# Moving the transfers that prepare the paired weights, and building the input sums in another place and on another engine

## The reference, cut to what matters

```python
def conv_ffn(x, prev, w_gate, w_up, w_dw, w_down):
    g = x @ w_gate
    g_ext = jnp.concatenate([prev.astype(g.dtype), g], axis=1)
    g_c = depthwise_causal_conv(g_ext, w_dw)
    y = (jax.nn.gelu(g_c, approximate=True) * (x @ w_up)) @ w_down
    return y, g_ext[:, -(FFN_CONV_WIDTH - 1):]
...
    f, st_f = conv_ffn(rms_norm(h, p['norm_ffn_pre'][layer]), ffn_prev[layer], ...)
    h = h + rms_norm(f, p['norm_ffn_post'][layer])
```

## Time and profile before

| | |
|---|---|
| median of 3 runs | 3144.06 us (3136.15 to 3147.18) |
| the profiled execution | 3141.24 us, span of the trace 3139.5 us |
| PE busy | 3004.6 us, 96% of the span |
| DVE, ACT, POOL busy | 1922.6, 1431.9, 518.0 us |
| granted PE clock, mean | 0.98 |
| transfers | 739.67 MB, mean 236 GB/s |
| queue of SP (q1), of POOL (q0) | 589.87 MB, 145.60 MB |

### The profile page before, as it was taken

The page is one execution under the profiler, slowest core; times in us unless marked ns, Lnnn a source line. Parts: engine busy times, 40 slices in busy tenths (PEclk is TensorE's granted clock), DMA queues, the critical chain, the costliest instruction groups (busy, mean ns, idle before and its releaser), DMA issues.

```text
span 3139.5 us, 62628 instructions
## 1 busy us (share of the span) xinstructions
PE 3004.6 (96%) x24274; PEld 2598.1 (83%) x24274; DVE 1922.6 (61%) x2846; ACT 1431.9 (46%) x2709; POOL 518.0 (16%) x738
## 2 busy tenths in 40 slices
PE   8999999899799999999999999999999899899999
PEld 7987887678799998998777777777887677799998
DVE  6998676544677445634666666666476653577532
ACT  5445632223355333323676777777443223255422
POOL 0211000010100101221333333333000010200100
PEclk9999999999899999999999999999999999999999
DMA  4323289986697535556999999999549996688632
GB/s 128 84 71 88 81 277 275 280 216 192 188 297 244 167 106 165 177 169 198 347 387 403 395 403 399 403 398 380 176 152 306 271 279 189 166 281 269 223 109 85
DMA packets 560090, 739.67 MB, mean 236 GB/s; under 512 B 29186, under 2 KB 407419, under 8 KB 559721
## 3 DMA queue, kind: packets, MB, share of 16 engines
q1 hardware_dynamic: 511318, 589.87, 55.0%
q0 software_dynamic: 48384, 145.60, 16.9%
q10 hardware_dynamic: 92, 0.19, 0.0%
HBM read 624.99 MB, written 172.04 MB: 254 GB/s over the span
## 4 chain that ended last, share of the span: by engine, by line
PE 68%; DVE 12%; DMA 12%; ACT 3%; issue 3%; SPq 0%; DVEq 0%; ACTq 0%
PE PS L1186 31%; PE PS L1638 11%; DMA raw<-in_ffn_w_up 7%; PE PS L2746 7%; PE PS L2782 4%; PE PS L2758 4%; DVE mT L989 4%; DVE wlo L417 3%; PE PS L2801 2%; DMA raw<-in_ffn_w_down 2%; PE PS L2820 2%; PE PS L2811 2%; ACT whi L412 2%; DMA weight_parts_kept<-wlo 1%; DVE cv L1899 1%
## 5 line engine op out<-in xcount | busy, mean ns | idle before, releaser
L417 DVE TENSOR_TENSOR wlo<-raw,whi 128x1024 fp32r<-128x1024 f32 (+1 forms) x300 | 359.5, 1198 | 698.6 <-ACT whi L412 690.8
L412 ACT CAST whi<-raw 128x1024 fp32r<-128x1024 f32 (+1 forms) x298 | 306.2, 1027 | 892.0 <-PE PS L1186 427.5
L1186 PE MATMUL PS<-xfh,whi 128*128 128x512 f32 (+3 forms) x1152 | 405.6, 375 | 80.1 <-DVE wlo L417 76.6
L1186 PE MATMUL PS<-xfh,wlo 128*128 128x512 f32 (+3 forms) x1152 | 398.4, 369 | 0.0
L1186 PE MATMUL PS<-xfl,whi 128*128 128x512 f32 (+3 forms) x1152 | 398.0, 368 | 0.0
L1186 PEld LDWEIGHTS PS<-xfh,whi 128*128 128x128 f32 x1152 | 213.7, 194 | 126.4 <-issue 91.7
L2746 PE MATMUL PS<-ident,kr 128*128 128x128 f32 x2048 | 277.2, 276 | 2.6 <-ACT kt L2916 2.6
L2746 PEld LDWEIGHTS PS<-ident,kr 128*128 128x128 f32 x2048 | 224.8, 141 | 39.0 <-issue 37.2
L3009 DVE COPY kt<-PS 128x512 f32<-128x512 f32 x256 | 172.6, 681 | 130.2 <-PE PS L2746 128.1
L1186 PEld LDWEIGHTS PS<-xfh,wlo 128*128 128x128 f32 x1152 | 212.5, 193 | 34.2
L1186 PEld LDWEIGHTS PS<-xfl,whi 128*128 128x128 f32 x1152 | 213.3, 194 | 32.8 <-issue 0.5
(11 more groups left out here) (444 smaller groups left out, 6695.0 us busy)
## 6 DMA issues: line engine op xcount, KB each, us to landing
kr<-in_cache_k SPq DMA_DIRECT2D x256, 512.0 KB, 7.5
vr<-in_cache_v SPq DMA_DIRECT2D x256, 512.0 KB, 7.2
raw<-in_ffn_w_down SPq DMA_DIRECT2D x64, 512.0 KB, 4.2
raw<-in_ffn_w_gate SPq DMA_DIRECT2D x54, 512.0 KB, 6.8
raw<-in_ffn_w_up SPq DMA_DIRECT2D x54, 512.0 KB, 7.7
extra_low<-weight_parts_kept SPq DMA_DIRECT2D x54, 512.0 KB, 5.8
weight_sums<-in_ffn_w_up POOLq DMA_DIRECT2D x24, 1088.0 KB, 10.9
weight_sums<-in_ffn_w_gate POOLq DMA_DIRECT2D x24, 1088.0 KB, 9.1
```

The lines of the kernel that those rows point to most:

```text
L412: nc.scalar.copy(whi[b][:, 0:blocks_of(t), :], raw[t % RAWS][:, 0:blocks_of(t), :]).then_inc(w_hi, 1)
L417: nc.vector.tensor_tensor(wlo[t % RAWS][:, 0:n, :], raw[t % RAWS][:, 0:n, :], whi[b][:, 0:n, :].bitcast(F32), ALU.subtract).then_inc(w_lo, 1)
L1186: mm = nc.tensor.matmul(PS[:, s + c, 0:c1 - c0], stationary(wt, t, kw + k), x(k0 + k)[:, c0:c1], start=start and k == 0 and wt is whi and ...
```

## The change

- Layer 0: of the 32 transfers of weight sums, 16 are issued in `out00` and `out01` (one after each tile, at the end of `glu_pool`), 11 in `up00` (at odd f), 5 in `down00` (n = 0 to 4).
- Layer 1: none in its own `up10` and `down10`. 16 are issued in `down01` (two after each `m_out` store), 16 in `kv0` and `kv1` (after every second tile).
- `x32` is no longer a tensor of its own but the place of half 1 in `hT`: `x_scaled` writes it there in `down` half 0, after a wait (at i = 14) for the stores of the residual. The 8 instructions of L1988 go.
- The four input sums are made by DVE instead of POOL, at the start of `up` half 1. ACT rounds two of them at f = 0 and two at f = 1; DVE makes two `t_lo` at f = 1 and two at f = 2; PE waits for each before the product that reads it.
- In `up` half 1 the residual update of half 0 (`post_part`) starts at f = 4 instead of f = 2, its loads on POOL likewise.

```diff
@@ -284,7 +284,7 @@
-    x32 = slots("x32", [P, KB, NH], F32, 32)
+    x32 = hT[:, :, AT0[1]:AT0[1] + NH]
@@ -959,6 +959,9 @@
             last_shifts(pool, 1, 1)
             states_stored(KB - 1)
             buffer_free(KB - 1)
+            for i in range(2 * KB):
+                pool.wait_ge(w_used, first["out00"] + i + 3)
+                weight_sum(pool, 0, i)
 
         def glu_dve(dve):
             def own(n=0):
@@ -1565,13 +1568,13 @@
+        SUM_ORDER = (0, 2, 1, 3)
-        def kept_count(layer, sums, rows):
-
-            return KEPT_OUT + 16 * ((SUMS + KB) * layer + sums + rows)
+        def rows_kept(layer):
+            return KEPT_OUT + 16 * KB * (layer + 1)
@@ -1611,7 +1614,9 @@
-                sp.wait_ge(kept_out, kept_count(layer, SUMS, KB))
+                sp.wait_ge(sums_made, 16 * SUMS * (layer + 1))
+                sp.wait_ge(kept_out, rows_kept(layer))
+                sp.wait_ge(sx_t, SX_T + 4 * (layer + 1))
@@ -1660,13 +1665,19 @@
+                if g == 0:
+                    pe.wait_ge(sx_l, SX_L + 4 * (layer + 1))
+            def sums_ready(n):
+                if g == 0:
+                    pe.wait_ge(sx_l, SX_L + 4 * layer + n)
+
+            sums_ready(1)
-                pe.wait_ge(sx_l, SX_L + 4 * (layer + 1))
@@ -1678,9 +1689,11 @@
+            sums_ready(2)
+            sums_ready(3)
@@ -1823,9 +1836,9 @@
-                if half == 1 and f == 1:
-                    act.wait_ge(sx_t, SX_T + 4 * (layer + 1))
-                    for n in range(4):
+                if half == 1 and f <= 1:
+                    for n in SUM_ORDER[2 * f:2 * f + 2]:
+                        act.wait_ge(sx_t, SX_T + 4 * layer + n + 1)
@@ -1865,6 +1878,17 @@
+            def input_sums():
+                b11, b12 = x32[:, 0:HK, 0:HC], x32[:, 0:HK, HC:NH]
+                b21, b22 = x32[:, HK:KB, 0:HC], x32[:, HK:KB, HC:NH]
+                dve.wait_ge(w_used, t0 + 2)
+                nc.vector.tensor_tensor(t32[:, 0], b12, b11, ALU.subtract).then_inc(sx_t, 1)
+                nc.vector.tensor_tensor(t32[:, 1], b12, b22, ALU.subtract).then_inc(sx_t, 1)
+                dve.wait_ge(sx_t, SX_T + 4 * layer + 1)
+                nc.vector.tensor_tensor(t32[:, 2], t32[:, 0], b22, ALU.subtract).then_inc(sx_t, 1)
+                dve.wait_ge(sx_t, SX_T + 4 * layer + 3)
+                nc.vector.tensor_tensor(t32[:, 3], b21, t32[:, 2], ALU.add).then_inc(sx_t, 1)
@@ -1906,8 +1930,8 @@
-                if f >= 2 and f % 2 == 0 and f // 2 - 1 < KB:
-                    k = f // 2 - 1
+                if f >= 4 and f % 2 == 0 and f // 2 - 2 < KB:
+                    k = f // 2 - 2
@@ -1983,10 +2007,7 @@
-                dve.wait_ge(w_used, t0 + 2)
-                for k in range(KB):
-                    nc.vector.scalar_tensor_tensor(out=x32[:, k, :], in0=hT[:, k, tokens(1)], scalar=vec[:, k, V_FFN_PRE + layer:V_FFN_PRE + layer + 1],
-                                                   in1=rs_x[:], op0=ALU.mult, op1=ALU.mult).then_inc(sx_x, 1)
+                input_sums()
@@ -2040,9 +2061,10 @@
-                if half == 1 and f == 1:
-                    for n_ in range(4):
-                        dve.wait_ge(sx_h, SX_H + 4 * layer + n_ + 1)
+                if half == 1 and 1 <= f < FS0:
+                    for i in range(2 * f - 2, 2 * f):
+                        dve.wait_ge(sx_h, SX_H + 4 * layer + i + 1)
+                        n_ = SUM_ORDER[i]
@@ -2109,6 +2131,7 @@
+            lo32 = x32 if half == 0 else lo32
@@ -2140,9 +2163,12 @@
+            lo32 = x32 if half == 0 else lo32
+                if half == 0 and i == 14:
+                    dve.wait_ge(kept_out, rows_kept(layer))
@@ -2174,10 +2200,11 @@
-                    if half == 0:
-                        for i in range(FB, SUMS):
-                            if (i - FB) * KB // (SUMS - FB) == n:
-                                weight_sum(pool, layer, i)
+                    if half == 0 and layer == 0 and n < 5:
+                        weight_sum(pool, 0, 27 + n)
+                    if half == 1:
+                        weight_sum(pool, 1, 2 * n)
+                        weight_sum(pool, 1, 2 * n + 1)
@@ -2196,12 +2223,12 @@
-            if i >= 1:
-                pool.wait_ge(kept_out, kept_count(layer, i, KB if i >= FB else 0))
+            if SUMS * layer + i >= 1:
+                pool.wait_ge(sums_made, 16 * (SUMS * layer + i))
-                pool.dma_start(to, of, accum_op=ALU.add).then_inc(kept_out, 16)
+                pool.dma_start(to, of, accum_op=ALU.add).then_inc(sums_made, 16)
-                pool.dma_start(to, of).then_inc(kept_out, 16)
+                pool.dma_start(to, of).then_inc(sums_made, 16)
@@ -2209,33 +2236,21 @@
-        def input_sums(pool, layer):
-            a11, a12 = x32[:, 0:HK, 0:HC], x32[:, 0:HK, HC:NH]
-            a21, a22 = x32[:, HK:KB, 0:HC], x32[:, HK:KB, HC:NH]
-            pool.wait_ge(sx_x, SX_X + KB * (layer + 1))
-            nc.gpsimd.tensor_tensor(t32[:, 0], a12, a11, ALU.subtract).then_inc(sx_t, 1)
-            nc.gpsimd.tensor_tensor(t32[:, 1], a12, a22, ALU.subtract).then_inc(sx_t, 1)
-            pool.wait_ge(sx_t, SX_T + 4 * layer + 1)
-            nc.gpsimd.tensor_tensor(t32[:, 2], t32[:, 0], a22, ALU.subtract).then_inc(sx_t, 1)
-            pool.wait_ge(sx_t, SX_T + 4 * layer + 3)
-            nc.gpsimd.tensor_tensor(t32[:, 3], a21, t32[:, 2], ALU.add).then_inc(sx_t, 1)
-
-                    pool.wait_ge(w_used, first[f"up{layer}0"] + 2 * f + 3)
-                    weight_sum(pool, layer, f)
+                    if layer == 0 and f % 2 == 1:
+                        pool.wait_ge(w_used, first["up00"] + 2 * f + 3)
+                        weight_sum(pool, 0, 16 + f // 2)
-                pool.wait_ge(sx_x, SX_X + KB * (layer + 1))
-                input_sums(pool, layer)
-                    if f % 2 == 1 and 2 <= (f + 1) // 2 < KB:
-                        parts_back_pool(pool, layer, 0, (f + 1) // 2, ring_e)
+                    if f % 2 == 1 and 2 <= (f - 1) // 2 < KB:
+                        parts_back_pool(pool, layer, 0, (f - 1) // 2, ring_e)
@@ -2389,6 +2404,8 @@
+                if n % 2 == 0:
+                    weight_sum(pool, 1, 16 + KB * half + n // 2)
```

More of the change, by code:

```diff
@@ L343, in yoco_step @@
         fs_pe, fs_v, st_out = sem("ffn_state_transposed"), sem("ffn_state_read"), sem("ffn_tail_stored")
-        sx_x, sx_t, sx_h, sx_l, SX_X, SX_T, SX_H, SX_L = l_xc, l_t, l_sq, l_m, 16, 16, 8, 2
+        sx_t, sx_h, sx_l, SX_T, SX_H, SX_L, sums_made = l_t, l_sq, l_m, 16, 8, 2, s_np
         s_ld, S_LD = [ld_x[2 + 2 * n:4 + 2 * n] for n in range(3)] + [[ld_x[8], n_sq]], 16
```

## The result

| | median us | lowest to highest | runs |
|---|---|---|---|
| before | 3141.43 | 3136.15 to 3147.18 | 4 |
| changed | 3086.72 | 3084.97 to 3096.84 | 4 |

Ratio 0.9832, 95% interval 0.9803 to 0.9861: 55 us faster. The forecast was 3063, with 3035 to 3107 as its range. The profiled execution took 3088.0 us (span 3086.3, mean clock 0.988).

A forecast was written before the change was run, and what follows sets the result against it. PE was busy 96%; 133 us lay over in six `up`/`down` stretches where loads, sums and stores of weight parts fill the transfers. Gains 95 less 10 and 4 make 81: 3141.2 to 3060, plus 2.8 to the median, 3063; range 3035 to 3107.

The forecast's parts named there:

- A: Whole kernel: likeliest case, gains of 95 us less 10 for hosts and 4 at start of `kv0`; 3063 us; chance 0.52.
- B: Hosts: contention moves along, 48 sums cost 1.2 us each, 58 in all; 3111 us; chance 0.14.
- D: `up` stretches: stores of weight parts alone hold PE, some 50 of 63 us stay; 3095 to 3115 us; chance 0.08.
- `up10`: `up` half 0, layer 1: all 22 sums leave, 4 us left over, transfer share 0.67; gain 26 us.
- `up00`: `up` half 0, layer 0: 11 of 22 sums leave, 14 of 33 us stay, share 0.86; gain 19 us.
- `down10`, `down00`: `down` half 0, both layers: 10 and 5 sums leave, 3 and 6 us left of 13 and 12; gain 16 us.
- Starts: Start of `up` half 1, both layers: 6 and 5 us left of 23.5 and 21.5; gain 34 us.
- Hosts `out` and `down01`: Stages taking moved sums, priced with `kv`: 0.2 us for each of 48 sums, 10 us lost (0 to 58).
- `kv`: Sums inside at 0.2 us each; at the start of `kv0` POOL 8 to 12 us late, costing 4 (0 to 12).
- Two signs: Sums in `down01` landing under 9.5 us; PE losing under 10 us in the start of `kv0`.
- rival E: `down01` and `kv`: POOL becomes the bound, 71 and 43 us lost, 114 against 95 gained; 3163 us; chance 0.04.
- Rival C: Hosts: load and sum share engines evenly, load stays under 8.5 us, hosts free; 3047 us; chance 0.18.

The follow-up runs named there:

- e1: Changed kernel with all transfers of sums back in their old places (`up` and `down` half 0), the other edits kept; 3114.68 us, ratio 0.9912.
- e6: Changed kernel with layer 0's sums 11 in `glu`, none in `up00`; layer 1's 12 in `down01`, 6 in `kv0`, 14 in `out10`/`out11`; 3071.47 us.
- e12: Changed kernel, all sums placed anew: 18 `glu`, 14 `out0`; layer 1: 6 `down00`, 12 `down01`, 4 `q0`, 10 `out1`; 3073.95 us.
- e7: Kernel before the change with one edit: the four input sums made by DVE instead of POOL; 3132.06 us, ratio 0.9965.
- e3: Changed kernel with layer 1's sums taken out of `down01`: 0 to 15 in `kv`, 16 to 31 in `out10` and `out11`; 3087.58 us.
- e5: Changed kernel with layer 1's sums moved: 12 in `down01`, 6 in `kv0` from tile 4 on, 14 in `out10` and `out11`; 3078.8 us.
- e9: As e6, but layer 1's sums 12 in `down01`, none in `kv`, 8 in `q0`, 12 in `out10` and `out11`; 3084.35 us, ratio 0.9817.
- e11: Changed kernel with two sums allowed under way at once, odd and even on two semaphores; placement and number kept; 3127.76 us, ratio 0.9956.

## Why the prediction was right, and where a term was off

The 3087 measured is inside the range of 3035 to 3107, but 2 us outside A's own, 3045 to 3085: it was the width left for B and D that held it. Against the profiled execution of before (3141.2) the gain is 53, where the sum gave 81.

- **`up10`**, gain 26: 27.4. The stretch of 241 lies in the forecast 240 to 250, its loads land after 3.7/4.0/7.5, share 0.67 as worked out. The stores of parts alone cost nothing; rival D falls (e1).
- **`up00`**, gain 19: 13.7, share 0.89 for 0.86. The 11 sums that stayed cost 16 (e6), and 19 are left over in all, not 14.
- **`down10`, `down00`**, gain 16: 11.2 and 3.0. `down00` keeps 9 of its 12, not 6. Of its five sums four add, and the residual's stores aren't needed for the loss: in e6 they go out during `up00` (574.7 to 578.4), and `down00` still takes 129, with loads of 6.8 to 10.5 us beside the adding sums. In e12, where they are out as well, six plain sums leave it at 121. So here the adding ones cost about 2 us each and the plain ones next to nothing, though the two runs also place them at other n.
- **Starts**, gain 34: 17.6 and 16.4, exactly 34. The wait fell to 1.1 and 1.4 (forecast 1 to 4). That POOL's sums held DVE is shown by e7, and this step alone is worth 8 of the 34. The other 26 came with the eight scalings that went, the divided `t_lo` and the later `post_part`; e1 shows that they owe nothing to the placement, but no run takes them apart.
- **Hosts `out` and `down01`**, 6.4 of the 10: 3.4 and 1.5. The first is inside the spread of that stretch. PE is idle there for 2.9 and 1.3 us, under the 5 named.
- **`kv`**, 3.2 of the 10 and 4 for the start: **32.8**. This is the mis-sized term, 26 of the 28 us missing; `up00` adds 5, and smaller differences of both signs make up the rest. Two signs named in the prediction point at it: sums in `down01` were to land under 9.5 us and PE to lose under 10 at the start of `kv0`; five adding sums there took 8.7 to 12.1, and PE was idle for 15.

The mechanism at the start of `kv0` was told rightly in part: POOL late, ACT held by key stores (14.6), DVE waiting for `ring_g` (6.1). The longest wait isn't in it, ACT's 16.9 us for the last `m_out` store, nor is it said there that the stores themselves would land so late beside an adding sum (12.2 and 9.9 us). Its size came from "the four adding pairs take 2 x 9.1, 1.5 more than a block each". The 9.1 is the median of seven adding and four plain sums together. Adding ones took 10.7 here (the four of the chain), a pair 21.4 against a block of 16.7. By that, POOL falls 4.7 behind in each of four blocks, 19 us and not 8 to 12; in the trace the eight take 85 us from the first issue to the last landing, where four blocks last 67. The start cost about 19 instead of 4. For the inside of `kv`, 0.2 a sum leaned on the earlier trace rows, read as loads and sums alone. They aren't alone there: twelve stores of weight parts are issued in that stretch, the last at 632.7, and three of its four sums are plain. `kv` has as many adding as plain ones, and key stores, row stores, `ring_g` loads and the residual beside them, and loads landed after up to 16 us (e3). The term of rival E, "in `kv` a sum and the stores behind it take 15.3 against 12.6 for two tiles", 43 us, was nearer than that of A; it stood under the slower case and was left out of the likeliest. It is near by luck: its mechanism, POOL as the bound inside `kv`, isn't what the trace shows, where POOL waits for sums only 14 us in all after 1200.

Rival C was right for the hosts with few other transfers and wrong for `kv`. By the rule named with it (the Trainium skill, DMA: Bandwidth & Descriptors, section "Queues, rings and completion order"), a load beside a sum takes at most about double, 8.2 us, as the prediction estimated from it. The medians in `out` and `down01` agree, 5.1 and 5.9, the longest don't, 10.1 in both. The estimate also took the packets of the two queues as equal, and they aren't: from 1047 to 1165 the profile counts 4867 packets with 15.41 MB on POOL's queue, 3.2 KB each, and 19369 with 9.75 MB on SP's, 0.5 KB each. Turns by packet between such queues don't keep a load within double, so the longest landings speak against the estimate and not against the rule.

What stays open: which of `kv`'s own transfers makes it so much dearer than `down01`, whose share is 0.81 against 0.90 to 0.94. No run took the key stores or the residual away. Nor is it settled why 10 to 16 sums in `out10` and `out11` cost between 7 and 17 us over there and in `up10`.

## What to carry to other kernels

A background transfer isn't priced by the mean share of the transfer engines, but by its own length against the pace of the stage, and by what stands behind it in its issuer's queue: find the longest kind (here those that add), take that kind's rows apart from the others, and compare with the time between two issues. Price a host by a row with the same number of streams; if there is none, take the bound from the case with more streams and not from the one with fewer. Spreading does not make bytes free: e5, e6, e9 and e12 each gave back in other stages half or more of what they won in `up00`, `down00` and `kv`, and letting two go at once was the worst of all.

## What the hardware showed that was not expected

- From DRAM to DRAM (1088 KB) a sum that adds takes over half longer than a plain one beside the same loads. In the output projection of the changed kernel, eight plain ones (295 to 349) and five adding ones (349 to 392); the third row is five adding ones at the end of `down01` (1130 to 1190):

```profile
DMA to landing us min/median/max: 5.4/5.6/6.7
...
DMA to landing us min/median/max: 8.6/8.9/10.1
...
DMA to landing us min/median/max: 8.7/11.7/12.1
```

- With two sums at once on POOL's queue the longest weight load was longer though the bytes are the same, in one trace of each: in the output projection its landings went from the first of these rows (changed) to the second (e11). The median fell, the longest doubled:

```profile
DMA to landing us min/median/max: 3.9/5.1/10.1
```

```profile
DMA to landing us min/median/max: 4.1/4.3/19.7
```

- POOL's four sums stretched DVE's four convolution steps from 1.74 to 11.39 us, each engine working on its own data in SBUF. The Trainium skill (SBUF — State Buffer, section "Who interferes with whom") says that a DVE instruction with two SBUF inputs contends with a GpSimd instruction that reads SBUF; e7 agrees: 11.39 became 1.74 when POOL's four went.
